# Stationary-weight products of a transformer kernel that walk their 256 columns from the last to the first

## What is computed

```python
def _swiglu(x, w_gate, w_up, w_down):
    return (jax.nn.silu(x @ w_gate) * (x @ w_up)) @ w_down

for l in range(DEPTH):                       # 2
    x = x + 0.5 * _swiglu(_rmsnorm(x, ffn1_norm[l]), ffn1_w_gate[l], ffn1_w_up[l], ffn1_w_down[l])
    h = _rmsnorm(x, mix_norm[l]); z = h @ w_in[l]
    ...
    x = x + merged @ w_out[l]
    x = x + 0.5 * _swiglu(_rmsnorm(x, ffn2_norm[l]), ffn2_w_gate[l], ffn2_w_up[l], ffn2_w_down[l])
for i in range(DEPTH_2):                     # 4
    x = x + mix
    x = x + mem_cross_attention(rmsnorm(x, norm_cross[i]), mem_n, ca_w_q[i], ca_w_kv[i], ca_w_o[i])
    x = x + swiglu(rmsnorm(x, norm_ffn[i]), ffn_w_gu[i], ffn_w_down[i])
```

## Time and profile before

| | |
|---|---|
| median of the runs | 2871.64 us (2869.03 to 2883.26) |
| span of the profiled execution | 2878.8 us |
| TensorE matmul busy | 2822.3 us (98%), 24,180 matmuls |
| TensorE weight load busy | 2771.7 us (96%) |
| GpSimd busy | 2108.9 us (73%) |
| ScalarE busy | 1333.4 us (46%) |
| VectorE busy | 1066.5 us (37%) |
| mean DMA rate | 173 GB/s |

### The profile page before, as it was taken

The page is one execution under the profiler, slowest core; times in us unless marked ns, Lnnn a source line. Parts: engine busy times, 40 slices in busy tenths (PEclk is TensorE's granted clock), DMA queues, the critical chain, the costliest instruction groups (busy, mean ns, idle before and its releaser), DMA issues.

```text
span 2878.8 us, 55910 instructions
## 1 busy us (share of the span) xinstructions
PE 2822.3 (98%) x24180; PEld 2771.7 (96%) x24180; DVE 1066.5 (37%) x1865; ACT 1333.4 (46%) x1490; POOL 2108.9 (73%) x462
## 2 busy tenths in 40 slices
PE   8999999999999999999999999999999999999998
PEld 8999889999999899999999998999999999999998
DVE  4217534213155443445333144333123331453331
ACT  5335544344355454345443484444354443454442
POOL 6777657878876578776768783659886688767785
PEclk9999999999999899999999999999999999999999
DMA  7974344555554355554445542445554455544553
GB/s 231 193 198 170 135 144 176 191 185 188 199 184 152 112 192 189 182 185 147 168 169 191 191 177 87 158 144 197 191 204 153 147 195 196 191 147 161 176 192 116
DMA packets 74197, 496.88 MB, mean 173 GB/s; under 512 B 8399, under 2 KB 13135, under 8 KB 14968
## 3 DMA queue, kind: packets, MB, share of 16 engines
q1 hardware_dynamic: 68344, 485.88, 46.9%
q10 hardware_dynamic: 5632, 7.62, 2.7%
HBM read 490.05 MB, written 3.41 MB: 171 GB/s over the span
## 4 chain that ended last, share of the span: by engine, by line
PE 86%; POOL 4%; DMA 3%; issue 3%; DVE 2%; ACT 2%; ACTq 0%; SPq 0%; POOLq 0%; DVEq 0%
PE G L454 21%; PE G L456 21%; PE G L455 21%; PE S L454 5%; PE S L456 5%; PE S L455 5%; POOL wl L400 4%; DMA raw<-w_units 2%; PE G L691 1%; PE S L1042 1%; ACT wh L1113 1%; DMA bias<-tables 0%; PE S L842 0%; PE S L799 0%; PE S L805 0%
## 5 line engine op out<-in xcount | busy, mean ns | idle before, releaser
L400 POOL TENSOR_TENSOR wl<-raw,wh 128x2048 fp32r<-128x2048 f32 x458 | 2108.7, 4616 | 740.5 <-ACT wh L1113 719.0
L1113 ACT ACTIVATE wh<-raw 128x2048 fp32r<-128x2048 f32 x456 | 873.7, 1918 | 1045.6 <-DMA raw<-w_units 1045.5
L454 PE MATMUL G<-ah,wl 128*128 128x256 f32 x4304 | 1209.2, 281 | 15.6 <-DVE wl L1768 8.9
L455 PE MATMUL G<-al,wh 128*128 128x256 f32 x4304 | 1200.6, 279 | 0.0
L456 PE MATMUL G<-ah,wh 128*128 128x256 f32 x4304 | 1200.3, 279 | 0.0
L454 PEld LDWEIGHTS G<-ah,wl 128*128 128x128 f32 x4304 | 816.4, 190 | 24.1 <-issue 15.1
L455 PEld LDWEIGHTS G<-al,wh 128*128 128x128 f32 x4304 | 815.2, 189 | 0.6
L456 PEld LDWEIGHTS G<-ah,wh 128*128 128x128 f32 x4304 | 814.1, 189 | 0.0
L454 PE MATMUL S<-gh,wl 128*128 128x256 f32 x1408 | 391.4, 278 | 3.4 <-POOL wl L400 3.4
L455 PE MATMUL S<-gl,wh 128*128 128x256 f32 x1408 | 391.3, 278 | 0.0
L456 PE MATMUL S<-gh,wh 128*128 128x256 f32 x1408 | 391.2, 278 | 0.0
(11 more groups left out here) (371 smaller groups left out, 3786.3 us busy)
## 6 DMA issues: line engine op xcount, KB each, us to landing
raw<-w_units SPq DMA_DIRECT2D x459, 1024.0 KB, 4.8
bias<-tables ACTq DMA_DIRECT2D x24, 128.0 KB, 3.2
tables<-trow ACTq DMA_DIRECT2D x12, 192.0 KB, 9.0
con<-consts SPq DMA_DIRECT2D x1, 1056.0 KB, 16.8
x<-x_in SPq DMA_DIRECT2D x4, 256.0 KB, 5.8
raw<-w_units SPq DMA_DIRECT2D x4, 256.0 KB, 6.9
memx<-mem_in ACTq DMA_DIRECT2D x1, 1024.0 KB, 7.4
out<-full SPq DMA_DIRECT2D x4, 256.0 KB, 2.5
```

What stands on the lines that cost most here:

```text
L400: pool.tensor_tensor(wl[:, j * UW:(j + 1) * UW], raw[:, j * UW:(j + 1) * UW], wh[:, j * UW:(j + 1) * UW].bitcast(F32), ALU.subtract)\
L454: pe.matmul(out, sl, vh, start=start and k == 0, stop=False, **kw)
L455: pe.matmul(out, sh, vl, start=False, stop=False, **kw)
L1113: act.activation(wh[:, j * UW:(j + 1) * UW], raw[:, j * UW:(j + 1) * UW], ACT.Copy)\
```

## The change

A new helper `mirrored` reverses the last dimension of the output and of both moving operands; the stationary operands stay. It is put around the operands of `product` in the five places where a weight is stationary. As input and output are reversed alike, each token's result lands where it did.

```diff
+            def mirrored(out, parts):
+                return out[:, ::-1], [(sh, sl, vh[:, ::-1], vl[:, ::-1]) for sh, sl, vh, vl in parts]
...
 (features)
-                        ins = product(out[:, fc * col:fc * col + T], parts, k == 0, k == KD - 1)
+                        ins = product(*mirrored(out[:, fc * col:fc * col + T], parts), k == 0, k == KD - 1)
...
 (features_by_input)
-                        ins = product(out[:, fc * 256:fc * 256 + T], parts, k == 0 and fc == 0, k == KD - 1,
+                        ins = product(*mirrored(out[:, fc * 256:fc * 256 + T], parts), k == 0 and fc == 0, k == KD - 1,
                                       skip_group_check=True)
...
 (down)
-                            ins = product(out, parts, first and kt == 0 and dc % 2 == 0,
+                            ins = product(*mirrored(out, parts), first and kt == 0 and dc % 2 == 0,
                                           last and kt == 1, skip_group_check=True)
...
 (the last two units of down)
-                            ins = product(out, parts, False, u == FP - 1, skip_group_check=True)
+                            ins = product(*mirrored(out, parts), False, u == FP - 1, skip_group_check=True)
...
 (branch_part)
-                        ins = product(outs[dc // 4][:, (dc % 4) * T:(dc % 4 + 1) * T], parts, True, True)
+                        ins = product(*mirrored(outs[dc // 4][:, (dc % 4) * T:(dc % 4 + 1) * T], parts), True, True)
```

## The result

| | before | changed |
|---|---|---|
| median of the runs, us | 2870.34 (2868.42 to 2883.26) | 2936.36 (2930.95 to 2940.64) |
| ratio | 1 | 1.0215, 95% interval 1.0185 to 1.0244 |
| span of the profiled execution, us | 2878.8 | 2938.7 |

By the medians the changed kernel is 66 us slower, by the ratio 2.15% (interval 1.85% to 2.44%). The spans of the two profiled executions differ by 59.9 us, and it is this difference that the traces have to account for. First the page of the changed kernel: busy times, the chain, and the product groups (columns as in the earlier trace rows; lines 454 to 456 have become 458 to 460).

A forecast was written before the change was run, and what follows sets the result against it. TensorE, which never rests, was taken to bound the kernel. Read, write and beat terms summed to 0 + 0 + 0 on the median, so 2872 us was forecast, range 2765 to 3000 us, leaving out the half rate.

The forecast's parts named there:

- The bound, the count, the price of a nanosecond: TensorE's matmuls bound the kernel; 20,208 of 24,180 matmuls change; one nanosecond per changed matmul is 20.2 us, 0.7%.
- Write backwards: nothing: Reversed PSUM output of the changed products: no cost taken, with less confidence; upper bound 216 ns per matmul.
- Half rate: Changed products' moving stream or write taken column by column: 2051 us more, 4923 us; chance 0.18.
- Read backwards: no cost of its own: Reversed SBUF read of the changed products' moving operand: no cost taken; upper bound one column in two clocks, 216 ns.
- The beats stay: Product stretches keep beats of 117.5 and 113.1 ns, only their mix can change: 2843 to 2932 us; chance 0.42.
- all slow: Upper end of the case that beats stay: all changed products at the slow beat, 61 us more, 2932 us.
- I take no net change: Mix of beats in the changed products: no net change taken, between 28 us saved and 61 us added.
- The smoother beat: Reversed moving reads of changed products stall less against stationary reads: 2843 to 2761, in the middle 2802 us; chance 0.25.
- The rougher one: In steady feed-forward stretches reads meet more often, 121.9 ns: 3021 us, for half the matmuls 2947; slower, chance 0.15.
- Moving-weight products keep 113 to 118: The 1920 unchanged products with moving weights should keep 113 to 118 ns in each case; otherwise the beat is carried over.

## Why the prediction was right, and where not

**The bound, the count, the price of a nanosecond** held: TensorE's matmuls carry the difference, and the sum of everything else stays within 1 us.

**Write backwards: nothing** held (0.9994). The Trainium skill's page "PSUM — Partial Sum Buffer", Specifications (TRN2), has any non-contiguous pattern slowing matmuls significantly; a step of -1 doesn't, at 2.4 GHz and float32. **Half rate** (4923 us) fell with it: the longest reversed beat in any sweep is 123.8 ns, not 216. **Read backwards: no cost of its own** held only in this sense: with the 352-byte pad the reversed read wins. At the kernel's own place it has a cost, and the term was put at nothing from rows of step 0 in another form, which can't show it.

**The beats stay** (0.42) comes nearest in number, not in mechanism. Its words were that both beats survive and only their mix changes. The measured 2936.4 us is 4 us above that case's own end, "all slow", 2932 us. For the changed products the traces have 57 us (12,770 x 4.44), where "all slow" had 61, and 2.5 us for the moving-weight products, which it did not count. But the fast beat did not survive in the changed products, and neither did the rhythm of the slow one: the reversed read brought a beat of its own. That its mean is 117.8 ns, the same as the slow beat's, belongs to this place; at most other places in the sweeps it is 120.0. That the result lies this near to a priced case is luck. The stated range of 2765 to 3000 us holds it easily, but it was wide because it spanned cases of both signs.

**The step that failed is "I take no net change".** I called the beat chance, with eight stages to draw for, and priced the two ends, but gave the point forecast to the middle. The change didn't draw anew; it took the fast beat away. The prediction also says that "the code doesn't choose the beat". With `down` alone reversed, and with the pad at 0, the two parts of one stage have different beats in one execution, 113.3 and 117.8 ns in the one, 120.0 and 113.3 in the other: place and direction decide which beats there are, and only the choice among those is left to what ran before. My second paragraph had a hint. L1054 at 109 and L691 at 112 ns on other buffers spoke for a beat that hangs on how the two reads lie, and a pad of exactly 192 bytes in the code suggests that a good place had been looked for. A change of the walk through the buffers then has more to lose than to win. How rare the good places are, only the sweep showed.

The smoother beat (0.25) needed a better place and there was none. The rougher one (0.15) had the right mechanism, reads that meet otherwise, but the wrong size: it put the new beat one step above the slow one, at 121.9 ns, and it came at 117.8. Its sign was a count under 1015 per 120 us, that of the forecast 1021 to 1062; the changed kernel has 1016 to 1022, partly in between, so the signs did not separate the two as I had meant. A beat above the slow one is what the forward kernel with 352 bytes shows (1.0333).

**Moving-weight products keep 113 to 118** held by the numbers but not as I meant it: they lost the fast beat too, as it is handed on from the stretch ahead. That is 570 x 4.4 = 2.5 us. They can still take it by themselves: with the input alone reversed, one stretch of them that began after an interruption was fast (191 matmuls at 113.3 ns).

What stays open: why places meet badly. That only TensorE takes part is shown (no other engine runs in the sweeps), and that it is the read and not the write (output alone reversed changes nothing). That the moving read and the weight load collide in SBUF is my inference; no row has a name for it. The Trainium skill's page "TensorE: Matmul & The Clock Gate", Part 2, speaks against it: it says that loading the next weights doesn't steal read bandwidth from the running matmul. Here the same stream of loads and matmuls takes 113.3 to 123.8 ns according to place and direction alone, and the measurement decides on the time, not on its cause.

## What to carry to other kernels

If matmuls of 256 columns alternate with loads of 128 in float32r, read the distance of their starts, not their duration, and look for several fixed beats; between the two of this kernel lie 4% of such a stretch. A mean doesn't tell beats apart: look at single distances too. Before judging a change that alters addresses or direction, sweep the place of the moving operand against the stationary one in a kernel of products alone (a few hundred segments, 1.4 ms): it foretold two whole kernels to 3 us and a third to 9. Then move the operands exactly as in the sweep: with both at other places than there it was 115 us off.

## What the runs showed of the hardware that I had not expected

- The distance of two matmuls depends on the place of the moving operand relative to the stationary one, modulo 256 bytes, and on the place of the stationary one (16 bytes change it, 32 and 64 nearly not): 113.3 to 123.4 ns forwards, 117.7 to 123.8 reversed.
- At one place there can be two beats, 113.3 and 117.8 ns. Which one is taken depends on what ran just before (at the kernel's place after three f32 matmuls always the fast one, after four always the slow one), and with operands of one kind it lasts over up to 1500 matmuls until the next interruption. From forward products to moving-weight ones it is handed on (12 of 12 places), back from those it changes to the other beat (9 of 9 in three kernels).
- A reversed output costs nothing (0.9994, 0.9967 to 1.002).
- The spread of the runs is not the draw of the fast beat alone. The kernel before spreads over 20 us in thirteen runs. Without a fast beat the two kernels with 352 bytes have 2.6 and 2.8 us over three runs each, but the changed kernel has 10 us over four and the kernel with the weights 16 bytes up 15 us over six.
